# Token-major norm statistics, gates applied early and GpSimd in the block loops of a two-layer diffusion trunk, with the modulation pieces moved out of the gaps

## What is computed

```python
for l in range(DEPTH):                      # DEPTH = 2
    m = (silu(c) @ w_mod[l] + b_mod[l])     # nine vectors of 1024 (N_MOD), for the latent and the context stream
    h = h + 0.5 * m[2] * rms_norm(ffn(modulate(h, g[0], m[0], m[1])), g[1])     # d_ff = 2816
    u = modulate(h, g[2], m[3], m[4])
    y = token_mixing(u)                     # u @ w_in (3256 columns); MLA, neighbourhood attention, gated
    h = h + m[5] * rms_norm(y, g[3])        # DeltaNet, Mamba-2 SSD; concatenated @ w_out
    h = h + 0.5 * m[8] * rms_norm(ffn(modulate(h, g[4], m[6], m[7])), g[5])
```

## Time and profile before

| | |
|---|---|
| median of 3 runs | 2689.05 us (2689.0 to 2689.52) |
| the profiled execution's own time | 2683.14 us |
| its span in the profile | 2681.4 us |
| mean granted TensorE clock | 0.909 |
| instructions | 29935 |
| modulation pieces | 72, of them 25 in the gaps |

### The profile page before, as it was taken

One profiled execution on the slowest core, in us unless ns is written; L12 is line 12 of the kernel. 1 busy time (PEld: TensorE's weight loads), 2 busy tenths in 40 slices (PEclk: granted clock), 3 DMA queues, 4 the chain that ended last, 5 costly groups with the idle time before them and its releaser, 6 DMA issues. The chain is left out here.

```text
span 2681.4 us, 29935 instructions
## 1 busy us (share of the span) xinstructions
PE 2305.6 (86%) x12457; PEld 1870.2 (70%) x12457; DVE 1226.1 (46%) x1773; ACT 816.1 (30%) x1248; POOL 86.6 (3%) x99
## 2 busy tenths in 40 slices
PE   4899999799885586899999899999799872877997
PEld 2578888487554575678888578888588551766997
DVE  0422334852546546643334643334644546446555
ACT  1422221532233412242122232222333233313443
POOL 0000000000000310000000000000000000400000
PEclk9899999899787777999999899999889876878998
DMA  7253423422222012342432532432423210025572
GB/s 240 87 144 107 111 75 106 127 89 83 69 63 79 1 48 95 113 107 70 127 89 76 157 89 71 117 97 84 143 73 110 73 63 0 1 63 169 160 196 88
DMA packets 403175, 258.89 MB, mean 97 GB/s; under 512 B 21834, under 2 KB 401760, under 8 KB 403040
## 3 DMA queue, kind: packets, MB, share of 16 engines
q1 hardware_dynamic: 403040, 256.97, 33.0%
HBM read 255.89 MB, written 1.05 MB: 96 GB/s over the span
## 5 line engine op out<-in xcount | busy, mean ns | idle before, releaser
L674 PE MATMUL bank<-uh,wh 128*128 128x512 f32 (+1 forms) x1536 | 565.0, 368 | 38.8 <-DVE ul L1523 25.0
L676 PE MATMUL bank<-uh,wl 128*128 128x512 f32 (+1 forms) x1536 | 558.4, 364 | 0.0
L675 PE MATMUL bank<-ul,wh 128*128 128x512 f32 (+1 forms) x1536 | 558.3, 363 | 0.0
L1468 DVE TENSOR_TENSOR wl<-ring,wh 128x2048 fp32r<-128x2048 f32 (+1 forms) x160 | 323.8, 2023 | 157.2 <-ACT wh L1127 156.4
L1127 ACT ACTIVATE wh<-ring 128x2048 fp32r<-128x2048 f32 (+1 forms) x160 | 270.9, 1693 | 319.4 <-PE bank L676 281.9
L674 PEld LDWEIGHTS bank<-uh,wh 128*128 128x128 f32 x1536 | 293.4, 191 | 99.6 <-issue 41.6
L676 PEld LDWEIGHTS bank<-uh,wl 128*128 128x128 f32 x1536 | 293.6, 191 | 44.9
L675 PEld LDWEIGHTS bank<-ul,wh 128*128 128x128 f32 x1536 | 294.3, 192 | 42.7
L674 PE MATMUL bank<-hh,wh 128*128 128x512 f32 (+1 forms) x704 | 255.4, 363 | 0.0
L675 PE MATMUL bank<-hl,wh 128*128 128x512 f32 (+1 forms) x704 | 255.2, 362 | 0.0
L676 PE MATMUL bank<-hh,wl 128*128 128x512 f32 (+1 forms) x704 | 255.2, 362 | 0.0
(11 more groups left out here) (268 smaller groups left out, 3018.7 us busy)
## 6 DMA issues: line engine op xcount, KB each, us to landing
ring<-in_ffn_w_dram SPq DMA_DIRECT2D x176, 512.0 KB, 5.3
ring<-in_w_mod_dram SPq DMA_DIRECT2D x144, 512.0 KB, 4.6
ring<-in_ffn_w_dram SPq DMA_DIRECT2D x64, 384.0 KB, 3.4
ring<-in_ffn_w_dram SPq DMA_DIRECT2D x64, 320.0 KB, 4.1
ring<-in_w_in_dram SPq DMA_DIRECT2D x40, 512.0 KB, 4.7
ring<-in_w_out_dram SPq DMA_DIRECT2D x16, 512.0 KB, 7.2
ring<-in_w_in_dram SPq DMA_DIRECT2D x4, 544.0 KB, 4.5
ring<-in_w_in_dram SPq DMA_DIRECT2D x2, 1024.0 KB, 5.3
```

The lines of the kernel that those rows point to most:

```text
L674: pe.matmul(bank, w_hi, x_hi, start=first, stop=False)
L675: pe.matmul(bank, w_hi, x_lo, start=False, stop=False)
L676: return pe.matmul(bank, w_lo, x_hi, start=False, stop=last)
L1468: TT(low[:, b, 0:floats], at, high[:, b, 0:floats].bitcast(F32), ALU.subtract).then_inc(wl_ready, 1)
```

## The change

It edits five things at once.

1. *Statistics, token-major.* The squares become the weights of a matmul and two columns of ones move through it, 128 tokens at a time (`token_sums`), so that the sums of 512 tokens are four columns of one per partition. Square root and reciprocal run on four columns (`std`, `rst`). `spread` multiplies each column, broadcast over 128, with the identity, which gives the reciprocal root over all partitions in a PSUM bank; the scalings read it there.
2. *Gates early.* ACT multiplies each block of y by the gate as soon as it has been squared (`gain`), during the last down or output pieces, one instruction for each half of the tokens. The addition to `xT` is then one instruction over 512 tokens. `yacc` is no longer zeroed, and the last square goes to TensorE by itself. ACT touches the sqrt function once before the down pieces (`load_sqrt`), and rounds the next block's first piece before the postnorm (`round_next`).
3. *GpSimd* adds blocks 2 and 5 to `xT`, subtracts the low parts of the odd blocks, and the low part of the first piece of each block (`split_first`).
4. *First products interleaved.* The first up piece takes k by k with w1 and w3, the projection its first two units k by k. Separate buffers (`u_in`, `sq_in`) take the projection's operands, so that nothing is rounded twice.
5. *Pieces moved.* The gaps have none. The first FFN of layer 0 takes 9 in its first half and 3 in its second, the mixing 36 and 16.

The core of the diff (GpSimd's and the other engines' calls of the same helpers are left out):

```diff
-    MOD_PLAN = {("start", 0): 8, ("ffn", 0): 7, ("gap0", 0): 5, ("mix", 0): 21, ("gap1", 0): 5, ("gap2", 0): 5,
-                ("gap0", 1): 5, ("mix", 1): 11, ("gap1", 1): 5}
+    MOD_PLAN = {("start", 0): 8, ("ffn0", 0): 9, ("ffn1", 0): 3, ("mix", 0): 36, ("mix", 1): 16}
...
-        MIX_PIECES = ((0, 2, 2, 2, 1, 1, 1, 1, 1, 4), (0, 1, 2, 2, 1, 1, 0, 0, 0, 4))
+        MIX_PIECES = ((2, 3, 3, 6, 1, 1, 1, 1, 2, 7), (1, 2, 2, 2, 1, 1, 1, 0, 0, 6))
...
+            def spread(n, bank, tiles):
+                pe.wait_ge(inverse_ready, n + 1)
+                for i in tiles:
+                    last = pe.matmul(bank[:, i * P:(i + 1) * P],
+                                     rst[:, NORM_AT + i:NORM_AT + i + 1].to_broadcast([P, P]), ident,
+                                     start=True, stop=True)
+                last.then_inc(inverse_spread, 1)
+
+            def token_sums(bank, squares, tiles, first, last):
+                for i in tiles:
+                    done = pe.matmul(bank[:, 2 * i:2 * i + 2], squares[:, i * P:(i + 1) * P], ones[:, 0:2],
+                                     start=first and i == tiles[0], stop=last, skip_group_check=True)
+                return done
 
             def prenorm(l, j):
-                norm(6 * l + 2 * j, lambda m: sq[:, m, t0:T], KC,
-                     lambda m: pe.wait_ge(x_squared, 8 * (3 * l + j) + m + 1), t0)
+                for m in range(KC):
+                    pe.wait_ge(x_squared, 8 * (3 * l + j) + m + 1)
+                    done = token_sums(ps[PRE_BANK], squares_of(j)[:, m, :], tiles, m == 0, m == KC - 1)
+                done.then_inc(sums_ready, 1)
+                spread(n, ps[PRE_BANK], tiles)
...
+                        order = [(g, k) for k in range(KC) for g in range(2)] if fresh else [
+                            (g, k) for g in range(2) for k in range(KC)]
...
-                A(rms[:, t0:T], ps[5][:, t0:T], ACT.Sqrt, bias=epsc[:, 0:1], scale=1.0 / D).then_inc(rms_ready, 1)
-
-            def round_in_place(l, m):
-
-                act.wait_ge(ul_ready, split_before(l, 1) + m + 1)
-                A(uTh[:, m, :], uT[:, m, :], ACT.Copy).then_inc(uTh_ready, 1)
...
+            def gain(l, j, m, hs):
+                act.wait_ge(y_sq, KC * q + m + 1)
+                for h in hs:
+                    y = uT[:, m, h * HALF:(h + 1) * HALF]
+                    last = A(y, y, ACT.Copy, scale=gpost[:, j, m, h:h + 1])
+                last.then_inc(y_gained, 1)
+
+            def load_sqrt():
+                A(small[:, 60:61], epsc[:, 0:1], ACT.Sqrt)
...
+                    if part == PARTS - 1:
+                        load_sqrt()
                     for j in range(KC):
...
+                        else:
+                            round_next(l, 2 * f)
+                        if part == PARTS - 1 and j:
+                            gain(l, 2 * f, j - 1, hs)
...
             def postnorm(l, j, hs):
                 for m in range(KC + 1):
                     if m < KC:
-                        TT(y(m), y(m), rms[:, t0:T], ALU.mult).then_inc(y_scaled, 1)
-                    if m:
-                        dve.wait_ge(y_scaled, 8 * q + m)
-                        for h in hs:
-                            last = STT(xT[:, m - 1, o], y(m - 1)[:, a:a + HALF], gpost[:, j, m - 1, h:h + 1],
-                                       xT[:, m - 1, o], ALU.mult, ALU.add)
-                        last.then_inc(x_ready, 1)
+                        dve.wait_ge(y_gained, KC * q + m + 1)
+                        TT(y, y, ps[POST_BANK][:, t0:T], ALU.mult).then_inc(y_scaled, 1)
+                    if m and m - 1 not in POOL_ADDS:      # POOL_ADDS = (2, 5)
+                        dve.wait_ge(y_scaled, KC * q + m)
+                        TT(x, x, uT[:, m - 1, t0:T], ALU.add).then_inc(x_ready, 1)
...
             def split_rest(n, floats, parts=(wh, wl)):
                 dve.wait_ge(wh_ready, SPLIT[n] + 1)
+                if n - 1 in FIRST_PIECES:
+                    dve.wait_ge(wl_ready, SPLIT[n])
...
+            def split_first(n, floats, parts=(wh, wl)):          # on GpSimd
+                pool.wait_ge(wh_ready, SPLIT[n] + 1)
+                pool.wait_ge(wl_ready, SPLIT[n])
+                G.tensor_tensor(low[:, b, 0:floats], ring[:, n % RING, 0:floats],
+                                high[:, b, 0:floats].bitcast(F32), ALU.subtract).then_inc(wl_ready, 1)
+
+            def low_rest(l, j, t0, u, high, low):                # on GpSimd
+                for m in range(1, KC, 2):
+                    pool.wait_ge(uh_ready, split_before(l, j) + m + 1)
+                    G.tensor_tensor(low[:, m, t0:T], u[:, m, t0:T], high[:, m, t0:T].bitcast(F32), ALU.subtract
+                                    ).then_inc(ul_pool, 1)
```

More of the change, by code:

```diff
@@ L146, in trunk @@
         MOD_PIECE += PIECES[place]
+    FIRST_PIECES = [PIECES[name][0] for name in PIECES if name[0] in ("up0", "in")]
     def ffn_mod(l, f, part, j):
@@ L225, in trunk @@
         silu_t = view(27648, 2, T)
-        ysq = silu_t[:, 0, :]
-        rms = silu_t[:, 1, :]
+        sq_in, u_in = view(8192, KC, T), view(0, KC, T)
+        ul_spare = view(7680, T)
         yacc = view(28672, T)
@@ L636, in mod_work @@
                         mod_turn(g, bank(g))
[L638 to L645, removed]
-            def prenorm(l, j):
-                t0 = HALF * pre_halves(l, j)[0]
-                norm(6 * l + 2 * j, lambda m: sq[:, m, t0:T], KC,
-                     lambda m: pe.wait_ge(x_squared, 8 * (3 * l + j) + m + 1), t0)
@@ L657, in gap @@
+            def postnorm(l, j):
+                tiles = tiles_of(post_halves(l, j))
+                n, q = 6 * l + 2 * j + 1, 3 * l + j
+                pe.wait_ge(y_summed, (KC - 2) * (q + 1))
+                token_sums(ps[POST_BANK], yacc, tiles, True, False)
+                pe.wait_ge(y_sq, KC * (q + 1))
+                token_sums(ps[POST_BANK], ysq_of(j), tiles, False, True).then_inc(sums_ready, 1)
+                spread(n, ps[POST_BANK], tiles)
             def gap(l, j):
-                m = gap_pieces(l, j)
@@ L716, in proj, with product @@
             def proj(l):
-                for n, (kind, j, c0, w, dest) in enumerate(UNITS):
+                def product(n, k):
+                    kind, j, c0, w, dest = UNITS[n]
                     t0 = first_of(l, dest)
@@ L721, in proj @@
                         c0, w = 256, w - 256
-                    if n == 0 or j != UNITS[n - 1][1]:
+                    bank, pw, b = ps[n % 4], IN_WIDTH[j], SPLIT[PIECES["in", l][j]] % 2
+                    ws = slice(k * pw + c0, k * pw + c0 + w)
+                    w_parts = wh_in[:, b, ws], wl_in[:, b, ws]
+                    if kind == "fm":
+                        return split_product(bank[0:w, t0:T], w_parts, (uTh[:, k, t0:T], ul_in[:, k, t0:T]),
+                                             k == 0, k == KC - 1)
+                    ts = slice(kind * P, (kind + 1) * P)
+                    return split_product(bank[:, 0:w], (uTh[:, k, ts], ul_in[:, k, ts]), w_parts,
+                                         k == 0, k == KC - 1)
+                pe.wait_ge(wl_ready, SPLIT[PIECES["in", l][0]] + 1)
+                for k in range(KC):
+                    wait_low(pe, l, 1, k)
+                    for n in range(2):
+                        last = product(n, k)
+                        if k == KC - 1:
+                            last.then_inc(proj_ready, 1)
+                pe.drain().then_inc(pieces_done, 1)
+                for n in range(2, NU):
+                    j = UNITS[n][1]
+                    if j != UNITS[n - 1][1]:
                         pe.wait_ge(wl_ready, SPLIT[PIECES["in", l][j]] + 1)
@@ L1039, in store @@
             def store():
-                pe.wait_ge(x_ready, 8 * 3 * LAYERS)
+                for m in range(KC):
+                    wait_x(pe, 3 * LAYERS - 1, m)
                 for t in range(2):
@@ L1401, in out_proj @@
                             A(uh[:, m, t0:T], uT[:, m, t0:T], ACT.Copy).then_inc(uh_ready, 1)
+                    for m in range(2 * j - 4, 2 * j - 2):
+                        if m >= 0:
+                            gain(l, 1, m, hs)
+                round_next(l, 1)
+                for m in range(2 * OUT_PIECES - 4, KC):
+                    gain(l, 1, m, hs)
             def store():
@@ L1921, in out_proj @@
                 split_rest(PIECES["out", l][0], 2048)
-                for m in range(KC):
+                for m in range(0, KC, 2):
                     dve.wait_ge(uh_ready, split_before(l, "out") + m + 1)
```

226 lines of the change are left out of this document (119 added, 107 removed).

## The result

The changed kernel takes 2718.51 us (median of 4 runs, 2715.68 to 2721.62) beside 2689.03 of the kernel before (four runs, one at 2670.1 and three at 2689.0 to 2689.52), a ratio of 1.0127, 95% interval [1.0081, 1.0173]. A second comparison gave 2720.84 beside 2683.02 (17 runs), 1.0136 [1.0121, 1.0152]. It is slower by 29 to 38 us, where 7 were forecast, and 5.5 us outside the stated range. The profiled execution has a span of 2714.9 us, 33.5 more than before, and a mean granted clock of 0.900.

A forecast was written before the change was run, and what follows sets the result against it. TensorE was taken as the bound, its gaps and half-clock time winnable. Gaps -29, feed -19 and moved pieces +55 sum to +7, so 2683.14 becomes 2690 profiled; with the median 5.9 higher, 2696 us, range 2682 to 2713.

The forecast's parts named there:

- Gaps, -29: Five gaps between blocks, plus start and end: token sums replace long `ones` products, 64 passes in 13.6 us; 29 us won.
- Rival 1: Token sums in the five gaps run at 2.4 GHz: 39 us less, 2657, faster; chance 0.07.
- Feed, -19: First products of blocks and projections: interleaving k and dropping double rounding cut feeding waits and slow clock, 19 us won.
- VectorE needs some 1.25 (half of the low parts are GpSimd's): First products: VectorE's time per k, in us, beside TensorE's six matmuls of 1.4 at full clock, 2.6 at half.
- a wait of 9.7 per layer: Projection: TensorE's wait and the slow clock in it shrink to a rest of about 4, winning 5.3 twice.
- I take 0 beyond what stands above: GpSimd's shared SBUF path with VectorE: no further cost, TensorE's sums and slow start being later; up to 2 a gap for range.
- Rival 3: GpSimd and VectorE hold each other up, chiefly in first products, also in gaps: 17 us in all, 2713; chance 0.2.
- The moved pieces, +55: Modulation pieces moved from the gaps into FFN, projection end, attention, scan and mixing: 55 us more, bounds 40 to 68.
- The price of 1.96 a piece: After attention and at the end of the mixing: each further modulation piece takes 1.96 us.
- Rival 2: Scan and end of the mixing cover more of the pieces: 15 us less, 2681, faster; chance 0.13.
- 25 leave the gaps, where they cost nothing.: Old gaps: the 25 modulation pieces stood beside the long links, not on them, so cost 0 there.
- The median: Whole kernel: median of runs 5.9 us above the profiled execution, as before, so 2696 given from 2690.

The follow-up runs named there:

- experiment 4: Changed kernel with prenorm squares rounded, one pass per token sum: 2686.96 us; with extra 128x256 matmuls between sums: 2748.97; with 128 columns moved instead of two: 2694.89.
- experiment 5: Changed kernel with pieces back in the gaps and squares rounded: 2660.62 us with GpSimd's share on VectorE, 2670.62 with it kept; feature-major prenorm sums, pieces between: 2635.07.
- experiment 2: Changed kernel with GpSimd's share of the block loops on VectorE: 2700.77 us; with only the odd low parts there: 2705.32; changed kernel beside them: 2720.84.
- Experiment 1: Kernel before with only the modulation pieces moved: 2731.22 us beside 2681.98; changed kernel with the pieces put back: 2702.44.

## Why the prediction was wrong

The sign was right and so was the place, the moved pieces against the gaps. The size was not: +33.5 by the two profiled executions, where the sum said +7. The stages show which terms failed: of the 26.5 missed, 9.4 lie in the feed term (the overlap of VectorE and GpSimd, and a wait counted twice), 8.1 in the moved pieces, 5.2 in the gaps, and 3.8 in items that the sum does not have.

- **Gaps, -29.** Measured -23.8: the five gaps -24.3, the start +3.3 (1.5 forecast), the end -2.9. The four of 512 tokens came out at 26.7, 26.7, 28.1 and 28.3 for 26.4, 26.4, 28 and 28. The 64 passes took 13.81 for 13.6, and experiment 4 confirms that they set the gap. Of the gaps only the 256-token one was mis-sized, 17.3 for 15.2; the rest of this miss is the start.
- **Rival 1 (sums at 2.4 GHz), chance 0.07.** It did not happen, the clock was 0.50 in every stream of sums. The price was about right, though: the wide passes, which got the full clock late, won 26 of the 39.
- **Feed, -19.** Measured -9.6, against the kernel before with the same pieces (149.35 to 148.30, 157.14 to 154.05, 124.79 to 123.65, 124.77 to 123.69, 147.81 to 145.38, 68.67 to 67.85). The step "VectorE needs some 1.25 (half of the low parts are GpSimd's)" failed: two k took 3.38 with GpSimd and 3.04 without. Without GpSimd the feed gives about 14, and the 512-token FFN halves come out at 122.1 and 122.6, as forecast. The remaining 5 are mostly in the projection, where "a wait of 9.7 per layer" was misread: of the 19.4 us of the earlier trace rows, 7.34 and 7.49 stand at the ends of two gaps, ahead of the first matmul, and the earlier trace rows had counted them there. Only 4.6 lie inside the projections, so that 5.3 a layer was too much (3.1 and 2.4 came):

```profile
501.77 0.77 PE L674 MATMUL bank<-uTh,wh_in 128*128 128x512 f32 x1 [7.34 <-ACT uTh L1136]
```

```profile
1936.19 0.55 PE L674 MATMUL bank<-uTh,wh_in 128*128 128x256 f32 x1 [7.49 <-ACT uTh L1136]
```

- **GpSimd, "I take 0 beyond what stands above".** This step failed, and a term was put at nothing: GpSimd's share costs some 7 in the stages, 4 of them inside the feed's miss, and 10 (experiment 5) to 20 (experiment 2) in the medians. The prediction considered the hold-up only for instructions with two SBUF inputs, after the earlier trace rows, and left out the one with scalars, 0.41 to 1.34. GpSimd's eight additions take 1.66 each (group mean), for the 1.27 assumed. The reason given for the 0, that TensorE's sums and slow start are later, held in the 512-token gaps (26.70 with GpSimd in the second, 26.78 without) but not in the first products. Rival 3 gave 17 to this, at a chance of 0.2, with the place right and the instruction form wrong.
- **The moved pieces, +55.** Measured +63.1: FFN 12.9 for 13.5, the end of the projection and the wait ahead of the first latent attention 10.3 for about 10 by the two terms, after attention 9.8 for 9, scan 10.4 for 10 (18.6 in the second execution), layer 1 7.7 for 6.2. The largest part of the miss is the end of the mixing in layer 0, 11.1 for 6. The price of 1.96 a piece holds while the ring has pieces ready and the clock is up; the sixth waited for its DMA, it and the seventh ran at half clock, and 1.1 of the 11.1 comes behind the pieces, where GpSimd's low part stands ahead of the output product.
- **Rival 2 (the mixing covers more), chance 0.13.** It did not happen, neither the scan nor the end hid a piece.
- **"25 leave the gaps, where they cost nothing."** Experiment 1 shows that they cost 13.2 in the old gaps, 7.4 of them in the 256-token one. The sum does not suffer from it, as the gap's length was worked out afresh, but it hid the real comparison: a piece cost 0.5 in the old gap (13.2 / 25), 1.9 in the new one (47.1 / 25), and 2.5 where it was moved to (63.1 / 25).
- **The median.** Small unforeseen items, the output product of layer 1 +1.2 and the last down products +1.5, make up most of the rest. The forecast assumed that the changed kernel's runs lie above its profiled one as before's did; the four runs of the changed kernel lay around it.

## What to carry to other kernels

Work that stands in a gap is free only while another engine is the bound there. An edit that makes the gap shorter by giving TensorE more to do has to be priced together with everything TensorE was hiding in it. And help from a second engine is priced with what it does to the first, for every instruction form of the first, not only for the form of which a slow example happens to be in the trace.

## What the runs showed that was not expected

- TensorE's clock went from 1.2 to 2.4 GHz inside a dense stream of weight loads with 128 moving columns each (0.50, then 1.00), in all six such streams of an execution. With two columns each it stayed at 0.50 over 13.8 us, and at 0.51 over 17 us with a 128x256 matmul after every eight passes.
- A pass with 128 columns took no longer than one with two: 0.22 at the lower clock for both, and at the upper 0.11 for 128 columns and 0.12 for two.
- A VectorE instruction with one SBUF input and two scalars per partition was held up by GpSimd to three times its length, 1.34 for 0.41, so that sharing the work made the pair of engines slower than VectorE alone.
- The attention of layer 0, the same instructions in every kernel, took 65.8 to 73.9 us with its granted clock between 0.95 and 0.84, in executions of one kernel too.
